# A mixture-of-experts stage packed into ten row blocks in place of eleven, with three fixed experts and a seventh weight buffer

## The reference, cut to what matters

```python
scores = sigmoid(t @ w_router); sel = scores + router_bias
best = argmax(sum of the top 2 of sel within each group of 4 experts)
idx = top 2 experts of the best group;  w = scores[idx] / sum
hid = silu(t @ w_gate[e]) * (t @ w_up[e])        # D_FF = 256, for each of 16 experts
out = sum over the two chosen experts of w * (hid @ w_down[e])
```

| layer | tokens of experts 0, 1, ..., 15 | experts 0, 1, 2 | the others by falling count |
|---|---|---|---|
| first | 38 35 30 51 43 30 42 31 99 72 105 52 45 13 45 37 | 38, 35, 30 | 105, 99, 72, 52, 51, 45, 45, 43, 42, 37, 31, 30, 13 |
| second | 57 50 46 37 21 24 31 26 48 76 62 38 69 49 47 87 | 57, 50, 46 | 87, 76, 69, 62, 49, 48, 47, 38, 37, 31, 26, 24, 21 |

## Time and profile before

### The profile page before, as it was taken

The page is one execution under the profiler, slowest core; times in us unless marked ns, Lnnn a source line. Parts: engine busy times, 40 slices in busy tenths (PEclk is TensorE's granted clock), DMA queues, the critical chain, the costliest instruction groups (busy, mean ns, idle before and its releaser), DMA issues. The chain is left out here.

```text
span 799.5 us, 9607 instructions
## 1 busy us (share of the span) xinstructions
PE 743.1 (93%) x3542; PEld 374.4 (47%) x3542; DVE 328.9 (41%) x870; ACT 216.1 (27%) x491; POOL 142.9 (18%) x238
## 2 busy tenths in 40 slices
PE   3999998999998999999899999888999899999994
PEld 1456653545446444443344755344544654444331
DVE  2023534735536453212272252564643744331136
ACT  2210255734023110111312025493411311101121
POOL 4146041120010200000112404122000120000102
PEclk9999999999999999999999999999999999999998
DMA  8997228899601999999897233345420399999961
GB/s 321 387 342 250 95 106 295 308 362 403 240 0 80 374 392 420 421 424 423 312 389 245 88 105 112 108 170 228 155 105 1 121 420 377 418 425 422 422 241 79
DMA packets 66340, 211.56 MB, mean 265 GB/s; under 512 B 7883, under 2 KB 8755, under 8 KB 54003
## 3 DMA queue, kind: packets, MB, share of 16 engines
q1 hardware_dynamic: 52744, 179.33, 57.9%
q10 hardware_dynamic: 7851, 17.70, 5.8%
q0 software_dynamic: 5696, 13.89, 4.8%
HBM read 202.02 MB, written 13.93 MB: 270 GB/s over the span
## 5 line engine op out<-in xcount | busy, mean ns | idle before, releaser
L2212 PE MATMUL bank<-ring,work 128*64 128x512 f32 (+1 forms) x512 | 156.5, 596 | 4.1 <-DMA ring<-in_w_up_dram 3.2
L2212 PEld LDWEIGHTS bank<-ring,work 128*64 128x64 f32 (+1 forms) x512 | 58.6, 157 | 96.2 <-issue 94.6
L2228 PE MATMUL bank<-ring,xs_tok 128*64 128x512 f32 (+1 forms) x256 | 79.9, 597 | 2.5 <-DVE xs_tok L1567 1.4
L1567 DVE COPY xs_tok<-bank 128x256 f32<-128x256 f32 x22 | 9.3, 425 | 150.7 <-PE bank L2219 150.7
L1850 PE MATMUL bank<-hT,ring 128*128 128x384 f32 x192 | 62.2, 486 | 0.0
L1724 PE MATMUL bank<-ring,cpad 128*32 128x512 f32 x384 | 48.6, 632 | 6.2 <-DMA ring<-in_w_ada_dram 5.4
L1850 PEld LDWEIGHTS bank<-hT,ring 128*128 128x128 f32 x192 | 36.5, 190 | 25.0
L2228 PEld LDWEIGHTS bank<-ring,xs_tok 128*64 128x64 f32 (+1 forms) x256 | 28.3, 157 | 39.6 <-issue 36.9
L984 ACT ACTIVATE xs_tok<-bank 128x256 f32<-128x256 f32 x22 | 8.5, 386 | 138.4 <-PE bank L2212 138.4
L2108 PE MATMUL bank<-ring,xn 128*128 128x512 f32 x96 | 43.6, 597 | 0.0
L991 ACT ACTIVATE qkv<-bank 128x512 f32<-128x512 f32 x40 | 21.7, 595 | 80.0 <-PE bank L2228 80.0
(11 more groups left out here) (389 smaller groups left out, 1062.1 us busy)
## 6 DMA issues: line engine op xcount, KB each, us to landing
ring<-in_w_ada_dram SPq DMA_DIRECT2D x48, 1024.0 KB, 8.9
ring<-in_w_gate_dram SPq DMA_DIRECT2D x32, 1024.0 KB, 8.2
ring<-in_w_up_dram SPq DMA_DIRECT2D x32, 1024.0 KB, 12.3
ring<-in_w_down_dram SPq DMA_DIRECT2D x32, 1024.0 KB, 10.9
ring<-in_w_in_dram SPq DMA_DIRECT2D x16, 1024.0 KB, 14.4
ring<-in_w_out_dram SPq DMA_DIRECT2D x8, 1024.0 KB
y_exp<-qkv ACTq DMA_DIRECT2D x16, 512.0 KB, 8.1
xpad<-gate_rows ACTq DMA_DIRECT2D x6, 512.0 KB, 5.7
```

Of the source, the lines that this page charges most:

```text
L1567: dve.tensor_copy(hidT[:, b, :], bank[2][:, 0:F]).then_inc(s_htc, 1)
L2212: last = mm(bank[b][i * n:(i + 1) * n, :].rearrange("p (i f) -> p i f", i=2), rows_T[:, kt * P + i * n:kt * P + (i + 1) * n], gate_up_of(s ...
L2228: last = mm(bank[5 + hf][i * n:(i + 1) * n, :], hidT[:, b, f * P + i * n:f * P + (i + 1) * n], w[:, f, hf * 512:(hf + 1) * 512], start=f = ...
```

## The change

It does these things, in both layers:

- FIXED = 3: experts 0, 1 and 2 are fixed, with 96 slots each (`FIXED_CAP`). 13 experts are ranked.
- Capacities by rank: the highest 128 (`FULL = 1`), ranks 2 to 4 get 96 (`WIDE = 4`), the nine others 64. These add up to 1280 slots, 10 full blocks, where there were 1408 in 11.
- An expert may be split over two blocks, and a block holds up to three parts (64, 32 and 32 columns); `gate_up` and `down` take lists of parts.
- A buffer `extra` over `xn` and `xpad`, which now lie side by side in `arena`, is a seventh place for units of the MoE. SP waits for `s_h` and `s_x1` before the first unit of a layer goes there. Landing semaphores are counted by 7 (`LANDED`), and both norm-weight semaphores are one.
- Units in a new order: gate-and-up of experts 0, 1, down of that pair, gate-and-up of expert 2 and the half of the next down unit that holds expert 2 come before SP's wait for `order`; the other half comes after it.
- Results are stored by expert (`stores_of`, up to three stores to a block) into 896 rows in place of 1024.
- On VectorE the selections of block 1 come after `order`; on TensorE the filler products stand before `lists(1)` (8 groups) and no longer behind it (10); DVE's `weighted(0)` comes after the last block's work.

```diff
-FIXED = 2
+FIXED = 3
-SLOTS = 6
+SLOTS, EXTRA, LANDED = 6, 6, 7
-PAIRS = ("fixed", "light", "heavy", "light", "heavy", "light", "light", "light")
...
+FULL, WIDE = 1, 4
+FIXED_CAP = 96
+RANK_OF = [None if _x < FIXED else _r for _x, _r in zip(range(E), (0, 0, 0, 1, 0, *range(2, RANKED)))]
+cap_of = lambda r: CAP if r < FULL else HALF + CAP // 4 if r < WIDE else HALF
...
+Q = CAP // 4
+wide = lambda x: ((x, 0, HALF), (x, HALF, Q))
+BLOCKS = [parts_of(*wide(0), (1, 0, Q)),
+          parts_of((1, Q, HALF), (2, 0, HALF)),
+          parts_of(*wide(3), (2, HALF, Q)),
+          parts_of((4, 0, CAP)),
+          parts_of(*wide(5), (6, 0, Q)),
+          parts_of((6, Q, HALF), (7, 0, HALF))] + [parts_of((x, 0, HALF), (x + 1, 0, HALF)) for x in (8, 10, 12, 14)]
...
+SPLIT = (1, 2)
+MOE_UNITS = [(0, 0), (0, 1), (1, 0), (0, 2), SPLIT]
...
+        extra = arena[:, DM:DM + UNIT]
...
                 for pair, k in MOE_UNITS:
-                    if pair not in experts:
+                    if (pair, k) == (SPLIT[0], 1):
                         sp.wait_ge(s_order, l + 1)
...
+                    if EARLIER[u] is not None:
+                        sp.wait_ge(*used(EARLIER[u]))
+                    else:
+                        sp.wait_ge(s_h, 16 * NT * (l + 1))
+                        sp.wait_ge(s_x1, 2 * NT * (l + 1))
...
-                    dve.memset(cap_row[:, 0:FIXED], float(CAP))
+                    dve.memset(cap_row[:, 0:FIXED], float(FIXED_CAP))
...
-                    step(dve.tensor_scalar(cap_row[:, FIXED:E], rank, float(HEAVY), float(HALF), ALU.is_le, ALU.mult))
+                    dve.tensor_scalar(cap_stored[:, FIXED:E], rank, float(FULL), float(Q), ALU.is_le, ALU.mult)
+                    step(dve.tensor_scalar(cap_row[:, FIXED:E], rank, float(WIDE), float(Q), ALU.is_le, ALU.mult))
                     dve.tensor_reduce(base_row[:, FIXED:E].unsqueeze(2), perm_tmp, AX.X, ALU.add)
-                    step(dve.tensor_scalar(cap_row[:, FIXED:E], cap_row[:, FIXED:E], float(HALF), None, ALU.add))
+                    step(dve.scalar_tensor_tensor(out=cap_row[:, FIXED:E], in0=cap_row[:, FIXED:E], scalar=float(HALF),
+                                                  in1=cap_stored[:, FIXED:E], op0=ALU.add, op1=ALU.add))
...
                 clock_kept(2, 2)
                 lists(0)
+                clock_kept(2, 8)
                 lists(1)
-                clock_kept(2, 10)
```

More of the change, by code:

```diff
@@ L60, with parts_of @@
     MOE_AT.append(len(ORDER))
-    assert len(ORDER) % SLOTS == 0
     ORDER += [("moe", MOE_U * _l + j) for j in range(MOE_U)]
-PAIRS = ("fixed", "light", "heavy", "light", "heavy", "light", "light", "light")
-BLOCKS = [(_p, _part) for _p, _kind in enumerate(PAIRS)
-          for _part in (((0, 1),) if _kind == "light" else ((0,), (1,)))]
-NB = len(BLOCKS)
[L69 to L74, removed]
+FULL, WIDE = 1, 4
+FIXED_CAP = 96
+RANK_OF = [None if _x < FIXED else _r for _x, _r in zip(range(E), (0, 0, 0, 1, 0, *range(2, RANKED)))]
+assert sorted(_r for _r in RANK_OF if _r is not None) == list(range(RANKED))
+cap_of = lambda r: CAP if r < FULL else HALF + CAP // 4 if r < WIDE else HALF
+def parts_of(*parts):
+    at, out = 0, []
+    for x, lo, n in parts:
+        out.append((x, lo, n, at))
+        at += n
+    assert at == CAP
+    return tuple(out)
+Q = CAP // 4
[6 more added lines that the diff above has]
+          parts_of((6, Q, HALF), (7, 0, HALF))] + [parts_of((x, 0, HALF), (x + 1, 0, HALF)) for x in (8, 10, 12, 14)]
+NB = len(BLOCKS)
+experts_of = lambda b: list(dict.fromkeys(x for x, *_ in BLOCKS[b]))
+pairs_of = lambda b: list(dict.fromkeys(x // 2 for x in experts_of(b)))
+for _x in range(E):
+    _cap = FIXED_CAP if RANK_OF[_x] is None else cap_of(RANK_OF[_x])
+    _held = sorted((lo, n) for parts in BLOCKS for x, lo, n, _at in parts if x == _x)
+    assert sum(n for _lo, n in _held) == _cap and all(a + n == b for (a, n), (b, _n) in zip(_held, _held[1:]))
+GU_BLOCK = [max(b for b in range(NB) if x in experts_of(b)) for x in range(E)]
 BUFS, HOTS = 4, 5
@@ L113 @@
         continue
+    _layer = max([at for at in MOE_AT if at <= _u], default=0)
     _holder = {s: max(v for v in range(_u) if SLOT[v] == s) for s in range(SLOTS)}
-    _s = min(_holder, key=lambda s: RELEASED[_holder[s]])
+    _last = [v for v in range(_layer, _u) if SLOT[v] == EXTRA]
+    if in_extra(_u):
+        _holder[EXTRA] = max(_last, default=None)
+    _s = min(_holder, key=lambda s: -1 if _holder[s] is None else RELEASED[_holder[s]])
     SLOT.append(_s)
@@ L2204, in rows_transposed, with gate_up @@
                     last.then_inc(done, 1)
-                def gate_up(b, rows_T, slots, done, between=None):
-                    n = P // len(slots)
+                def gate_up(b, rows_T, parts, done, between=None):
                     for kt in range(KT):
```

212 lines of the change are left out of this document (119 added, 93 removed).

## The result

| | before | after |
|---|---|---|
| median | 804.73 us | 1419.53 us (1418.74 to 1420.34) |
| ratio after to before | | 1.766, 95% interval 1.762 to 1.770 |
| span of the profiled execution | 799.5 us | 1418.6 us |
| TensorE busy | 93% | 74% |
| granted clock, mean | 0.994 | 0.874 |

The forecast was 1327 us with a range of 1200 to 1480. The time is inside, 92 us above the forecast: the kernel runs a round, as predicted, but two terms of the sum were off.

The account below looks back on a forecast made before the run. It took TensorE to bound the kernel, with the DMA engines about level. Profiled 801.2 us, less 20 gained, plus 543 for an overflow round, gave 1324 us, 1327 as median; range 1200 to 1480.

Parts of the forecast that it names:

- the gain: MoE stages of both layers: one block fewer and earlier weights save 20 us in all, bounds 12 and 23.
- The counts: First layer's router: 99 tokens against rank 2's 96 slots, 3 over, so one round over 16 experts; second layer nothing over.
- A step: One expert's pass in the overflow round, from slot sums to down product: 30.4 us, bounds 22.9 and 42.
- The loops' 1 us: Registers, branches and dynamic addresses in each step of the round: 1 us, bounds 0 and 3.
- The clock's 2.5 us: Gate-and-up product in a round step begins at a slow clock and ends fast: 2.5 us added, bounds 0 and 11.9.
- The round: After the first layer's blocks: 16 steps, 486 us, plus 57 us to get in and finish, 543 us together.
- the entry: Getting into the round after the first layer's blocks: 3 us.
- The DMA side of the gain: Weight supply of an MoE stage: earlier transfers and 1 MB less traffic end it 9.7 us earlier.
- Block 1's selections: Start of the MoE stage: they come about 1.5 us later, but block 0's first half runs in between.
- The clock stays at half: Rival, chance 0.18: round steps stay at half clock or loops cost, 39.8 us a step, about 1480 us.
- The weights alone bind: Rival, chance 0.15: in the round, gather and transposes end before weights land, 22.9 us a step, about 1190 us.
- No round: Rival, chance 0.05: nothing exceeds rank 2's capacity, only the saving is left, 784 us.

Follow-up runs that it names:

- the fillers: Changed kernel with unread filler products on TensorE during each round step's wait for gathered rows: 1469.72 us with 44 a step, 1372.95 us with 24.
- the light loads: Changed kernel whose round loads only 128 KB of each of a step's three weights, not 1 MB, computing with old ones: 1353.49 us.
- two experiments: Changed kernel running a round only for an excess over 128: 854.78 us; kernel before, made to enter a round with nothing over: 1368.77 us.

## Why the prediction was right, point by point

The mechanism was right: a round of 16 steps for 3 tokens makes nearly all of the change. That the time lies inside the range owes something to luck. The range of 1200 to 1480 us was made wide for steps of uncertain length, and the steps came out as forecast; 72 of the 92 us by which the forecast fell short come from the gain, which was given bounds of 12 and 23 us and had the wrong sign.

- **The counts.** Right. 3 tokens over a capacity of 96 start a round of 16 steps; without it the kernel takes 855 us. The gathers' bytes in the earlier trace rows had been enough to trust the reference's table.
- **A step, 30.4 us forecast.** Measured 30.4. The terms: issue 1.6 (1.7 forecast), gather 10.7 (10.1), transposes and copies 3.4 (2.6), gate and up 9.3 (7.0 + 2.5 for the clock), to the down product 1.9 (2.0), down 3.5 (3.5). The loops' 1 us is not there: the six terms already make up the period, with nothing left for registers, branches or a fetch of instructions. So the sum hit better than its terms: what the loops did not cost, the gather and the copies did. The clock's 2.5 us were 3, shown by the fillers; that 4.2 us of the gather's are due to the weights beside it was shown by the light loads.
- **The round, 543 us forecast.** 565 by two experiments. Of the missing 20 us 12 lie at the entry, for which 3 us stood: the first slot sums come 5.5 us after the last down product (426.1 to 431.6), and the first step takes 39.9 us (431.6 to 471.6), since its first product waits 14.9 us for weights. SP had 8 transfers of 1 MB of the next layer's input weights ahead of them. The other 15 steps took 30.7 us on the average and make 4 us more; store, result rows and gathers took 58 us, not 54.

```profile
457.20 8.95 PE L2289 MATMUL bank<-ring,hT 128*128 128x512 f32 x16 [14.87 <-DMA ring<-in_w_down_dram]
```

  That queue was in the code, behind the wait for `combined`, and was not counted.
- **The gain, 20 us forecast.** Wrong, and of the wrong sign: 52 us lost. The term is "three blocks with 24 such groups each make 0 to 5 us a layer; three weight loads are nearer to two than to four". It took the price of mixed widths from rows of one width, on either side, and believed that what lies between two cheap cases is cheap. Measured: 40 us a layer. In numbers of the forecast, 20 less the 77 that the parts cost more than taken is 57 us lost; the two stages grew by 57.3 us, and the whole kernel without the round lost 52. The bounds were bounds of something else.
- **The DMA side of the gain**, "the supply ends 9.7 us earlier": too simple. It counted bytes and the earlier start. Once the widths are mended and the capacities fit, the stage is 4 us shorter, not 10: TensorE waits 4.5 us for weights near the end, where two light experts to a block want more than the DMA engines bring. Whether that has to do with the buffers that are released early stays open.
- **Block 1's selections** were called covered by block 0's first half. With the fillers moved beside them they cost 5 to 6 us in all, about 3 of that through the clock (1.4 us in the first layer, 1.7 in the second): a filler and a wait are not the same thing.
- **The rivals.** "The clock stays at half" did not occur: gate and up are 9.3 us, not 14. "The weights alone bind" did not either: the first product of a step waits for the copies of the gathered rows, not for weights. "No round" was tried as an experiment and is slower than before, 855 us, not 784. So even that rival would have come out on the other side of the one it was priced for.

## What to carry to other kernels

A kernel with fixed capacities has a second program inside it for what does not fit, and a profile that never enters it shows none of its price. Before capacities are cut, hold the new ones against the counts of the data, and put a price on the overflow path, step by step from rows of the main path; it can be most of the answer. When a matmul block is split by columns, keep all parts in it of one width: here four of 32 cost the same as two of 64, and a mix of 64 and 32 cost more than twice as much.

## What the runs showed that was not expected

- Products of different column widths gained nothing from standing side by side: 64 + 32 + 32 columns interleaved take 15.95 us, one width after the other 14.07, where 32 x 4 or 64 x 2 take 7.05 and 7.04. Each change of width costs some 0.13 us more.
- The number of parts of one width has no price here, though the weight loads double in number. The earlier trace rows had suggested 0.506 us for a group of four against 0.44, but that mean is over short bursts of 16 instructions: most take 1.92 us, the one in the window at a clock of 0.53 took 3.22, and the first of the kernel 3.64.
- 128 gathered rows, nearly all of them the same one, land 4.4 us after the issue with idle DMA engines, 10.6 us after it beside 3 MB of weights and a store of 512 KB.
- Filling TensorE's wait with useless products was worth 47 us of 1420, as long as they end before the wait does; with fillers that ended 7 us after it in each step, the kernel was 50 us slower than with none.
